# Gated layer of a two-layer decoder step: the v product with the tokens as the stationary operand

## The chip, the cores and the metric

One core of one Trainium2 chip. The metric is the device time of one execution in microseconds (us); lower is better. TensorE is called PE in the rows (PEld its weight loads), VectorE DVE, ScalarE ACT, GpSimd POOL and SyncE SP.

## The reference, cut to what matters

Layer 0 of the two layers is the gated one. Its input is 1024 prompt tokens and 64 sample tokens of width 1024; `a` is 2048 wide.

```python
h = rmsnorm(x, g)                          # x * r * g, r = 1/sqrt(mean(x*x) + eps) of each token
u, v, z = split(h @ w_in, 3, axis=-1)      # w_in 1024 x 6144, each part 2048 wide
v = rmsnorm(v, g_v)                        # over the 2048 channels of a token
mixed = einsum('gts,bnsgd->bntgd', tril(w_s), v in chunks of 128 tokens) + b_s
y = u * mixed * silu(z)
x = x + y @ w_out
```

The sample tokens' normed v rows are an output of their own. All products are of fp32 precision: each operand is split into a high part (the value rounded to fp32r) and a low part (the rest), and three products are added up, high x high, low x high, high x low.

## The kernel before, in words

**Groups and units.** The gated layer runs over two groups of tokens: group 0 has the 64 sample tokens and prompt chunks 0 to 3 (576 columns, taken by PE as two halves of 288), group 1 has chunks 4 to 7 (512 columns). Weights come in units of 512 KB, 1024 elements a partition. Each unit goes through a two-deep ring: SP loads `wraw` (L602), ACT rounds it to `whi` (`split_hi`, L429), POOL subtracts to get `wlo` (`split_lo`, L434), PE multiplies (`gemm`, L446). `split_hi` of unit u waits for PE to be through with unit u-2 (`w_used`), and the load of unit u waits for `wlo` of unit u-2. A group has 16 units of v, then 32 of z and u in turn (z, u, then the spatial mixing of one 128-channel strip f, at L2047 and L2051), then 16 of w_out.

**The v product.** The weights are the stationary operand, so v comes out channel-major, 128 channels x n tokens, for each strip f. ACT takes it out of PSUM (`v_out_of_psum`, L925), PE turns it with 4 transposes, and a fifth for the sample tokens (L1992, L1998), and DVE stores the token-major result in `v_raw` (L1344, L1347). After the last strip ACT squares `v_raw` tile by tile over all 2048 channels to get the sums (L938), takes the root (L941), and DVE inverts it to `rv` (L1362), scales the sample rows for their output with `gvb` (L1365) and the first strip for the mixing (L1380).

**The start.** SP loads nine tiles of x (L616; `xearly` for tiles 0 to 4, which are group 0, `xlate` for 5 to 8). PE turns tiles 0 to 4 (L1961) and DVE copies them into `xT` (L1308). ACT squares the tiles (L883) and takes roots (L888); DVE inverts them and spreads them on a diagonal (L1314 to L1320), PE spreads that over the partitions (L456). Then for each of the 8 channel blocks k: DVE makes `hfa` = x * g * r (L553), ACT its high part `hhi_g` (L539), DVE its low part `hlo_g` (L559), and PE's first v unit goes block by block behind them. The four late tiles are turned in the v loop, two transposes a strip (L1995), and copied by DVE (L1351).

**POOL's queue.** It holds, in this order: constants, the small loads (`gn`, the factor g, at L738, and others), `split_lo` of unit 0, a wait for the last x tile (`x_in[8]`), the loads of `wsraw`, `bsb` and `gvb` (L752 to L755), `split_lo` of units 1 to 16, then a wait for the turned mixing weights (`ws_ev`), their causal mask (L770), eight small DMAs that build `wsbd` (L774), and `split_lo` of unit 17 and on. Unit 16 is the first z unit, unit 17 the first u unit.

Of the kernel before, what the change touches and what calls it, by code (L numbers as in the profile page):

```python
# [17 lines left out]
F32 = mybir.dt.float32  # L18
F32R = mybir.dt.float32r
# [7 lines left out]
P = 128  # L27
# [26 lines left out]

GROUPS = [(0, 576, 4, True, 2), (576, 512, 4, False, 1)]
# [63 lines left out]
def hybrid_trunk(nc, x_prompt, x_sample, cache_k, cache_v, cache_ik, page_table, p_prompt, p_sample,  # L119
# [5 lines left out]
    with ctx:  # L125
# [61 lines left out]
        hfa = pl("hfa", [P, 2, GW])  # L187
        sqa = rbc
        yhi = nc.alloc_sbuf_tensor_at("yhi", [P, KA, 5 * P], F32R, offset=V0)
        vtmp = [szt, t1a]  # L190
        pl = region(Y0, Y0 + KA * GW * 4)
        xlate = pl("xlate", [P, 4, D])
        sqdump = pl("sqdump", [P, D], BF16)
        vdump = nc.alloc_sbuf_tensor_at("vdump", [P, KA, P], F32, offset=Y0)
        v_out = nc.alloc_sbuf_tensor_at("v_out", [NS, AW], F32, offset=Y0 + KA * P * 4)
        wsraw = pl("wsraw", [P, NGRP, P])
        gvb = pl("gvb", [NS, AW])
        xearly = nc.alloc_sbuf_tensor_at("xearly", [P, 5, D], F32, offset=V0)
# [116 lines left out]
        def as3(ap):  # L315
# [9 lines left out]
        x_tr, x_sq, x_ev, x_rt, x_dg = (sem(n) for n in ("x_tr", "x_sq", "x_ev", "x_rt", "x_dg"))  # L325
        gn_in = sem("gn_in")
# [12 lines left out]
        gmlp = {n: sem(f"A_{n}") for n in ("vev", "vtr", "vst", "vsq", "rv", "vs", "mix", "mt", "sz", "ut",  # L339
                                           "y", "yhi", "ylo", "xup")}  # L340
        sA = [Turn(gmlp, {n: g * {"vsq": 5, "rv": 1, "xup": KD}.get(n, KA) for n in gmlp}) for g in range(2)]
# [80 lines left out]


# [173 lines left out]
        def _(sp):  # L597
# [13 lines left out]

            for j in range(9):
                c0, n = tile_cols(j)
                src = (x_sample.rearrange("b t d -> (b t) d") if j == 0
                       else x_prompt[0, CHUNK * (j - 1):CHUNK * j, :])
                sp.dma_start(xtile(j)[0:n, :], src).then_inc(x_in[j], 16)  # L616
                if j == 4:
                    unit(0, 0, slab(w_in_a[0], 0, AW))
                    unit(1, 1, slab(w_in_a[0], 0, AW + P))
            for g in range(2):  # L620

                with sp.Fori(1 if g == 0 else 0, KA // 2) as i:
                    for ff in range(2):
                        unit(ff, U_A[g] + 2 * i + ff, pair(w_in_a[0], AW, i, ff))
# [100 lines left out]
        def _(pool):  # L725
# [6 lines left out]
            nc.gpsimd.memset(sv[:], 1.0).then_inc(cst, 1)  # L732
            own.link(nc.gpsimd.memset(ident[:], 0.0))
# [21 lines left out]
            pool.dma_start(gvb[:], g_v_a[0].partition_broadcast(NS)).then_inc(gvb_in, 16)  # L755
# [6 lines left out]
            for g in range(2):  # L762
                c0, n, _, _, np_ = GROUPS[g]
                for base, trips in ((U_A[g], KA // 2), (U_A[g] + KA, KA)):
# [3 lines left out]
                    if base == 0:  # L768
                        pool.wait_ge(ws_ev, 2)
# [96 lines left out]
        def _(act):  # L866
            own = Tally(act, av)
            for name, free in (("vev", 2), ("sz", 1)):
                act.sem_inc(gmlp[name], free)
# [4 lines left out]
            act.wait_ge(cst, 7)  # L874
# [16 lines left out]
            def norm_act(act, s, hi):  # L891
                for k in range(KD):
                    norm_hi(act, s, k, *hi)
                    if k == 5:
                        split_hi(act, 1, 1, 1)
                    if k in (4, 6):
                        x_square(3 + k // 2)
                for j in range(7, 9):
                    x_square(j)

            for j in range(5):
                x_square(j)
            x_roots(0, 5)
            split_hi(act, 0, 1, 0)
# [8 lines left out]
            for g in range(2):  # L913
                c0, n, nch, has_s, np_ = GROUPS[g]
                h = n // np_
                s = sA[g]
                if g == 0:
                    norm_act(act, nA[g], group_hi(g))
                else:
                    split_unit(U_A[g] + 1)  # L920

                def v_out_of_psum(f, ff):
                    act.wait_ge(w_used, U_A[g] + f + 1)
                    act.wait_ge(s["vtr"], s.at("vtr", f + 1))
# [1624 lines left out]
```

## Time and profile before

| what | value |
|---|---|
| median of 3 runs (lowest, highest) | 1977.17 us (1976.70, 1978.89) |
| span of the profiled execution, first to last instruction | 1973.8 us |
| mean granted TensorE clock, as a share of 2.4 GHz | 0.975 |
| PE busy | 1863.0 us, 94% of the span |
| DVE, ACT, POOL busy | 862.2, 793.2, 649.9 us |

The runs agree within 0.11%. Of the profiled execution only the span is recorded; the median lies 3.4 us above it, which is taken as what lies around the span. The gated layer fills about the first 850 us: group 0's v product from 18 to 139 us, group 1's from 484 to 581 us.

### The profile page before, as it was taken

Reading aid. Unit: us, or ns where it says so; the run is one execution under the profiler, and the core shown is the slowest. Engines: PE = TensorE matmul, PEld = TensorE weight load, DVE = VectorE, ACT = ScalarE, POOL = GpSimd, SP = SyncE. Lnnn points to the kernel's source line nnn. Section 1 sums busy time; section 2 is a strip of 40 time slices with the busy share of each in tenths; the row PEclk is TensorE's granted clock in tenths of the full one; section 3 lists DMA queues with packets and bytes.
Section 4 is the critical chain, followed back from the end, with each engine's and each line's share of the span. In section 5 each row is a group of like instructions: output and inputs, shape, how many; then the busy total and the mean of one; then the engine's idle time right before and its main releaser. Section 6 shows DMA issues by size and latency. Waiting matters only on the chain. (4 is left out here: it accounts for less than half of the span.)

```text
span 1973.8 us, 30722 instructions
## 1 busy us (share of the span) xinstructions
PE 1863.0 (94%) x11000; PEld 1647.2 (83%) x11000; DVE 862.2 (44%) x1653; ACT 793.2 (40%) x1148; POOL 649.9 (33%) x397
## 2 busy tenths in 40 slices
PE   7999999899999999999979989999989998699998
PEld 7999999899887888779969549999966765499997
DVE  4113333311114444033254877687778634512433
ACT  4233333212243333233235675567865554402211
POOL 4333323265333334654522131111132002354220
PEclk9999999999999999999989899999999999899999
DMA  6223222222222222331123110312231006531111
GB/s 187 75 65 85 74 74 74 64 77 83 85 85 85 85 85 86 95 109 33 32 64 122 31 56 22 89 43 66 88 121 31 1 1 209 186 99 43 44 55 45
DMA packets 226179, 150.76 MB, mean 76 GB/s; under 512 B 16754, under 2 KB 219250, under 8 KB 225714
## 3 DMA queue, kind: packets, MB, share of 16 engines
q1 hardware_dynamic: 210754, 125.78, 21.6%
q0 software_dynamic: 5152, 14.48, 2.4%
q10 hardware_dynamic: 10192, 9.46, 1.4%
q8 instruction: 46, 0.75, 0.2%
q14 instruction: 35, 0.29, 0.1%
HBM read 133.24 MB, written 16.43 MB: 76 GB/s over the span
## 5 line engine op out<-in xcount | busy, mean ns | idle before, releaser
L434 POOL TENSOR_TENSOR wlo<-wraw,whi 128x1024 fp32r<-128x1024 f32 x177 | 430.2, 2431 | 722.4 <-ACT whi L429 720.3
L446 PE MATMUL PS<-hhi_g,whi 128*128 128x288 f32 (+1 forms) x1152 | 324.0, 335 | 12.2 <-POOL wlo L434 7.2
L429 ACT ACTIVATE whi<-wraw 128x1024 fp32r<-128x1024 f32 x177 | 186.6, 1055 | 343.0 <-PE PS L446 324.6
L446 PE MATMUL PS<-hhi_g,wlo 128*128 128x288 f32 (+1 forms) x1152 | 317.1, 330 | 0.0
L446 PE MATMUL PS<-hlo_g,whi 128*128 128x288 f32 (+1 forms) x1152 | 316.9, 329 | 0.0
L446 PE MATMUL PS<-hhi,whi 128*128 128x364 f32 x1176 | 269.7, 338 | 12.8 <-DVE hlo L559 6.8
L446 PE MATMUL PS<-hlo,whi 128*128 128x364 f32 x1176 | 262.0, 331 | 0.0
L446 PE MATMUL PS<-hhi,wlo 128*128 128x364 f32 x1176 | 260.6, 330 | 0.0
L446 PEld LDWEIGHTS PS<-hhi_g,whi 128*128 128x128 f32 x1152 | 195.7, 189 | 31.1 <-issue 6.6
L446 PEld LDWEIGHTS PS<-hhi,whi 128*128 128x128 f32 x1176 | 204.0, 191 | 20.4 <-issue 13.9
L446 PEld LDWEIGHTS PS<-hhi_g,wlo 128*128 128x128 f32 x1152 | 196.4, 189 | 17.7
L446 PEld LDWEIGHTS PS<-hlo_g,whi 128*128 128x128 f32 x1152 | 196.9, 190 | 16.2
L446 PEld LDWEIGHTS PS<-hlo,whi 128*128 128x128 f32 x1176 | 206.5, 190 | 0.0
L446 PEld LDWEIGHTS PS<-hhi,wlo 128*128 128x128 f32 x1176 | 206.3, 190 | 0.0
L446 PE MATMUL PS<-yhi,whi 128*128 128x288 f32 (+1 forms) x384 | 108.0, 335 | 5.3 <-POOL wlo L434 4.7
L1387 DVE TENSOR_TENSOR t2a<-PS,szt 128x576 f32<-128x576 f32 (+1 forms) x32 | 23.2, 725 | 198.9 <-PE PS L446 198.3
L446 PE MATMUL PS<-yhi,wlo 128*128 128x288 f32 (+1 forms) x384 | 106.0, 330 | 0.0
L446 PE MATMUL PS<-ylo,whi 128*128 128x288 f32 (+1 forms) x384 | 105.3, 329 | 0.0
L1626 DVE TENSOR_SCALAR_CACHE_REDUCE acc<-sc,thr 128x384 bf16<-128x384 f32 (+1 forms) x124 | 100.7, 812 | 4.1
L1344 DVE COPY v_raw<-PS 128x512 f32 x32 | 22.1, 691 | 176.7 <-PE PS L1998 91.2
L988 ACT ACTIVATE sig<-hfb 128x1092 f32<-128x1092 f32 x16 | 17.9, 1118 | 174.7 <-DVE hfb L1441 174.5
L1423 DVE TENSOR_TENSOR xT<-PS,xT 128x576 f32<-128x576 f32 (+1 forms) x16 | 11.6, 725 | 168.0 <-PE PS L446 168.0
(392 smaller groups left out, 2726.4 us busy)
## 6 DMA issues: line engine op xcount, KB each, us to landing
wraw<-in_w_in_a_dram SPq DMA_DIRECT2D x96, 512.0 KB, 3.9
wraw<-in_w_out_a_dram SPq DMA_DIRECT2D x32, 512.0 KB, 4.0
wraw<-in_w_in_b_dram SPq DMA_DIRECT2D x25, 512.0 KB, 3.7
wraw<-in_w_pe_gate_dram SPq DMA_DIRECT2D x16, 512.0 KB, 4.2
kpg<-in_cache_k_dram SPq DMA_DIRECT2D x64, 128.0 KB, 2.8
vpg<-in_cache_v_dram POOLq DMA_DIRECT2D x64, 128.0 KB, 2.4
xs<-xT SPq DMA_DIRECT2D x1, 4368.0 KB, 12.6
xT<-xs SPq DMA_DIRECT2D x1, 4368.0 KB, 14.0
```

The source lines that it names most:

```text
L429: nc.scalar.activation(whi[par][:], wraw[par][:], ACT.Copy).then_inc(w_hi, 1)
L434: nc.gpsimd.tensor_tensor(wlo[par][:], wraw[par][:], whi[par][:].bitcast(F32), ALU.subtract).then_inc(w_lo, 1)
L446: mm = nc.tensor.matmul(o, w[par][:, k, :], r(k, c0, cn), start=first and i == 0 and n == 0, stop=last and i == KD - 1 and n == 2)
L988: nc.scalar.activation(sig[:], tg, ACT.Sigmoid).then_inc(s["sig"], 1)
L1344: vdst = nc.vector.tensor_copy(v_raw[:, bass.ds(f, 1), 0:4 * P].rearrange("p o n -> p (o n)"), PS[:, 4 + 2 * ff, :])
L1387: nc.vector.tensor_tensor(t2a[:, 0:n].rearrange("p (b n) -> p b n", b=np_), PS[:, 2:2 + np_, 0:h], szt[:, 0:n].rearrange("p (b n) -> p b n ...
L1423: nc.vector.tensor_tensor(x, PS[:, b:b + np_, 0:h], x, ALU.add).then_inc(s["xup"], 1)
L1626: own.link(nc.vector.tensor_scalar(vdmp[:, 0:(b + 1) * P], area(b), thr[:, b - 2:b - 1], None, ALU.is_lt, ALU.add, accum_out=cnt[:, b - 2: ...
```

## The change

In both groups the v product is made token-major at once: a tile of 128 tokens (all 1024 input channels, in 8 blocks k) is the stationary operand and 512 columns of the weights move past it. The 2048 channels are done in four rounds r of 512; a round has four units, each with the weights of two blocks k and 512 columns, still 1024 elements a partition. One PSUM bank holds 128 tokens x 512 channels over the four units of a round. In group 0 the 64 sample tokens form a tile of their own, whose stationary operand is the high and the low part side by side (64 + 64 columns) in `vpair`, with two products instead of three; the upper 64 partitions of the result are added to the lower by ACT (`vlow`) and DVE.

Group 0's v product uses xg = x * g without r. DVE multiplies by r (per token, so per partition) as it takes v out of PSUM. The early tiles are copied by ACT instead of DVE, multiplied by g, and split, tile by tile. The normed `hhi_g`, `hlo_g` of group 0, which z and u need, are made in the third round; the late x tiles, the spreading of r and the turning of the mixing weights are put between v units, at bank 7. The squares of v are summed round by round. Group 1's v loop is written out on PE, ACT, DVE and SP. The load of `gvb` moves behind the last v unit. The diff, cut to its core:

```diff
+NRND = 4
+EARLY_BANK = (5, 3, 1, 5, 3)
...
+        def v_tiles(g):
+            return ([(4, NS)] if g == 0 else []) + [(c, P) for c in range(4)]
+        def v_bank(g, r, t):
+            return (5 * r + t) % 7 if g == 0 else (4, 5, 0, 1, 2, 3, 6, 7)[4 * (r % 2) + t]
...
 SP
+            def v_load(g, m):
+                u, r, q = U_A[g] + m, m // NRND, m % NRND
+                if u >= 2:
+                    sp.wait_ge(w_lo, u - 1)
+                src = w_in_a[0][2 * P * q:2 * P * (q + 1), AW + BANK * r:AW + BANK * (r + 1)]
+                sp.dma_start(v_weight(wraw, m), src.rearrange("(k p) c -> p k c", p=P)).then_inc(w_raw[m % 2], 16)
+            V_AFTER = {2: 0, 4: 1, 6: 2}
                 sp.dma_start(xtile(j)[0:n, :], src).then_inc(x_in[j], 16)
-                if j == 4:
-                    unit(0, 0, slab(w_in_a[0], 0, AW))
-                    unit(1, 1, slab(w_in_a[0], 0, AW + P))
+                if j in V_AFTER:
+                    v_load(0, V_AFTER[j])
...
 POOL
-            pool.dma_start(gvb[:], g_v_a[0].partition_broadcast(NS)).then_inc(gvb_in, 16)
                     if base == 0:
+                        pool.wait_ge(w_used, KA)
+                        pool.dma_start(gvb[:], g_v_a[0].partition_broadcast(NS)).then_inc(gvb_in, 16)
                         pool.wait_ge(ws_ev, 2)
...
 ACT, group 0 before the rounds
+                    early_copy(0)
+                    early_copy(1)
+                    early_hi(0)
+                    early_copy(2)
+                    early_hi(1)
+                    early_copy(3)
+                    split_unit(0)
+                    early_hi(2)
+                    early_copy(4)
+                    early_hi(3)
+                    early_hi(4)
+                    split_unit(1)
+                    for j in range(5):
+                        x_square(j)
+                    x_roots(0, 5)
+                    split_unit(2)
...
 ACT, both groups
-                    nc.scalar.activation(vdump[0:rows], v_raw[0:rows, :, c * P:(c + 1) * P], ACT.Square,
-                                         accum_out=sv[0:rows, c:c + 1]).then_inc(s["vsq"], 1)
+                for r in range(NRND):
+                    if has_s:
+                        v_done(act, g, r, 0)
...
+                        nc.scalar.activation(vlow[:], PS[NS:P, v_bank(g, r, 0), :], ACT.Copy,
+                                             scale=rxs[NS:P, 0:1]).then_inc(s["vlw"], 1)
+                    for t in range(nt - 1):
+                        v_square(r, t)
+                    split_unit(U_A[g] + NRND * r + 5)
+                    v_square(r, nt - 1)
+                    for m in range(6, 9) if r < NRND - 1 else ():
+                        split_unit(U_A[g] + NRND * r + m)
+                        if g == 0 and r == 1 and m >= 7:
+                            r_copy(m - 7)
+                        if g == 0 and r == 2:
+                            for k in range(3 * (m - 6), min(3 * (m - 5), KD)):
+                                norm_hi(act, nA[0], k, *group_hi(0))
...
 DVE
+            dve.wait_ge(gn_in, 32)
+            early_scale(0)
+            for j in range(1, 5):
+                early_scale(j)
+                early_lo(j - 1)
+            early_lo(4)
...
+                for r in range(NRND):
+                    if g == 0:
+                        for piece in ((0, 1), (2, 3, 4, 5), (6, 7), ())[r]:
+                            late_copy(piece)
+                    v_round(r)
+                    if g == 0 and r == 2:
+                        ws_copy(0)
+                        dve.wait_ge(x_ev, 7)
+                        for k in range(KD + 1):
+                            norm_tile(dve, nA[0], k, c0, n, *group_tile(0))
+                        ws_copy(1)
+                dve.wait_ge(s["vsq"], s.at("vsq", NRND * len(tiles)))
+                nc.vector.reduce_sum(sv[:], vsum[:], axis=AX.X).then_inc(s["rv"], 1)
...
 PE
+                        for kk in range(2):
...
+                            if rows == NS:
+                                x = vpair[:, k].rearrange("p h n -> p (h n)")
+                                products = ((x, hi), (x, lo))
+                            else:
+                                a, b = ((vhi, vlo), (hhi_g, hlo_g))[g]
+                                a, b = a[:, k, c * P:(c + 1) * P], b[:, k, c * P:(c + 1) * P]
+                                products = ((a, hi), (b, hi), (a, lo))
...
+                BETWEEN = {1: (late_transpose, 0), 2: (late_transpose, 1), 3: (late_transpose, 2), 4: (late_transpose, 3),
+                           5: (late_transpose, 4), 6: (late_transpose, 5), 7: (late_transpose, 6), 8: (late_transpose, 7),
+                           9: (r_spread, 0), 10: (r_spread, 1), 11: (ws_transpose, 0), 12: (ws_transpose, 1)}
+                for m in range(KA):
+                    v_unit(m)
+                    if g == 0 and m in BETWEEN:
...
                 if g == 0:
+                    pe.wait_ge(s["vst"], 18)
+                    pe.wait_ge(nA[0]["lo"], KD)
```

`v_transpose`, `v_out_of_psum` and the strip loops of v go. `late_transpose` is 4 transposes, `ws_transpose` is 4, `r_spread` one product of 288 columns, as many in all as before. `early_scale` multiplies a tile of x by g, `early_hi` and `early_lo` split it. `v_round` takes the tiles of a round out of PSUM.

## Rows read from the trace of the kernel before

**Rows 1.** The profile's page, its first row: busy time, share, instructions.

```profile
PE 1863.0 (94%) x11000; PEld 1647.2 (83%) x11000; DVE 862.2 (44%) x1653; ACT 793.2 (40%) x1148; POOL 649.9 (33%) x397
```

**Rows 2.** Timeline of PE, one v unit of group 0: start, length, instruction, releaser.

```profile
43.88 0.60 PE L1992 MATMUL PS<-ident,t1a 128*128 128x128 f32 x4
...
44.91 0.42 PE L446 MATMUL PS<-hlo_g,whi 128*128 128x288 f32 x2
...
50.99 0.60 PE L1992 MATMUL PS<-ident,szt 128*128 128x128 f32 x4
```

**Rows 3.** Timeline of PE, one v unit of group 1.

```profile
501.31 0.60 PE L1992 MATMUL PS<-ident,t1a 128*128 128x128 f32 x4
...
501.98 0.40 PE L446 MATMUL PS<-hlo_g,whi 128*128 128x512 f32 x1
...
507.35 0.60 PE L1992 MATMUL PS<-ident,szt 128*128 128x128 f32 x4
```

**Rows 4.** Timeline of all engines, the start.

```profile
3.70 1.99 POOL L738 DMA_DIRECT2D gn<-in_g_norm_dram  x2 [0.31 <-POOL wsbd L736]
...
13.66 1.06 ACT L429 ACTIVATE whi<-wraw 128x1024 fp32r<-128x1024 f32 x1 [1.22 <-DMA wraw<-in_w_in_a_dram]
...
18.25 0.82 PE L446 MATMUL PS<-hhi_g,whi 128*128 128x288 f32 x2 [2.58 <-DVE hlo_g L559]
...
23.43 0.75 DVE L559 TENSOR_TENSOR hlo_g<-hfa,hhi_g 128x576 fp32r<-128x576 f32 x1
...
23.66 0.90 POOL L752 DMA_DIRECT2D wsraw<-in_w_s_a_dram  x1 [6.51 <-DMA xlate<-in_x_prompt_dram]
...
25.67 2.38 POOL L434 TENSOR_TENSOR wlo<-wraw,whi 128x1024 fp32r<-128x1024 f32 x1
...
26.46 2.88 DVE L559 TENSOR_TENSOR hlo_g<-hfa,hhi_g 128x576 fp32r<-128x576 f32 x2
...
28.73 0.53 PE L446 MATMUL PS<-hhi_g,whi 128*128 128x288 f32 x2 [1.92 <-DVE hlo_g L559]
...
37.45 0.51 PE L446 MATMUL PS<-hhi_g,whi 128*128 128x288 f32 x2
```

**Rows 5.** The tile `gn` (g), its two loads: time from issue to landing.

```profile
DMA to landing us min/median/max: 6.2/6.3/6.5
```

**Rows 6.** Windows at the start: stretch, length, engines' busy time, PEclk, DMA share, GB/s.

```profile
20.00:22.00 2.00, 2.00 (x10) 1.94 (x9) 1.96 (x4) 0.68 (x1) 0.00 (x0) 0.50 1.01 392
```

**Rows 7.** The profile's page, DMA issues: size, median us from issue to landing.

```profile
wraw<-in_w_in_a_dram SPq DMA_DIRECT2D x96, 512.0 KB, 3.9
```

**Rows 8.** Timeline of all engines, group 0 from v to z and u.

```profile
138.89 0.51 PE L446 MATMUL PS<-hhi_g,whi 128*128 128x288 f32 x2
...
141.05 1.09 POOL L770 TENSOR_SCALAR_AFFINE_SELECT wsT<-wsT 128x1024 f32<-128x1024 f32 x1 [7.52 <-DVE wsT L1358]
...
149.38 0.52 PE L446 MATMUL PS<-hhi_g,whi 128*128 128x288 f32 x2 [3.90 <-POOL wlo L434]
...
150.62 2.34 DVE L1365 SCALAR_TENSOR_TENSOR v_out<-v_raw,rv,gvb 64x2048 f32<-64x2048 f32 x1
...
157.36 1.05 PE L2047 MATMUL PS<-wsT,vs 128*128 x8
...
159.29 0.53 PE L446 MATMUL PS<-hhi_g,whi 128*128 128x288 f32 x2 [0.52 <-POOL wlo L434]
```

**Rows 9.** Timeline of all engines, group 1: v begins, then from v to z and u.

```profile
484.07 0.39 PE L446 MATMUL PS<-hhi_g,whi 128*128 128x512 f32 x1
...
581.10 0.48 PE L446 MATMUL PS<-hhi_g,whi 128*128 128x512 f32 x1
...
593.46 1.15 PE L2047 MATMUL PS<-wsT,vs 128*128 x8 [0.93 <-DVE vs L1380]
...
597.37 0.79 PE L446 MATMUL PS<-hhi_g,whi 128*128 128x512 f32 x1 [2.76 <-POOL wlo L434]
...
600.48 0.39 PE L446 MATMUL PS<-hlo_g,whi 128*128 128x512 f32 x1
```

More of the change, by code:

```diff
@@ L616, in _ @@
                 sp.dma_start(xtile(j)[0:n, :], src).then_inc(x_in[j], 16)
[L617 to L619 removed]
+                if j in V_AFTER:
+                    v_load(0, V_AFTER[j])
             for g in range(2):
[L622 to L624 removed]
+                for m in range(3 if g == 0 else 0, KA):
+                    v_load(g, m)
                 with sp.Fori(0, KA) as i:
@@ L889, in x_roots, with early_copy, early_hi @@
                                      scale=1.0 / D).then_inc(x_rt, 1)
[L891 to L904, printed above, removed]
+            def early_copy(j):
+                c0, n = tile_cols(j)
+                b = EARLY_BANK[j]
+                act.wait_ge(x_tr, j + 1)
+                nc.scalar.activation(xT[:, :, c0:c0 + n], PSF[:, b * BANK:(b + 2) * BANK]
+                                     .rearrange("p (k t) -> p k t", k=KD)[:, :, 0:n], ACT.Copy).then_inc(x_ev, 1)
+            def early_hi(j):
+                n = tile_cols(j)[1]
+                act.wait_ge(x_g, j + 1)
+                nc.scalar.activation(early_part(vpair, vhi, 0, j), xg[:, j % 2, :, 0:n], ACT.Copy).then_inc(x_hi, 1)
             def split_unit(u):
@@ L916, in _ @@
                 s = sA[g]
+                tiles = v_tiles(g)
+                nt = len(tiles)
                 if g == 0:
-                    norm_act(act, nA[g], group_hi(g))
+                    early_copy(0)
[14 more added lines that the diff above has]
+                    split_unit(2)
+                    for j in range(5, 7):
+                        x_square(j)
+                    split_unit(3)
+                    for j in range(7, 9):
+                        x_square(j)
+                    split_unit(4)
@@ new lines, in r_copy, with v_square @@
+                def r_copy(c):
+                    a, m = group_cols(0)[c]
+                    act.wait_ge(nA[0]["sum"], c + 1)
+                    nc.scalar.activation(rbc[:, a:a + m], PS[:, 7, 0:m], ACT.Copy).then_inc(x_ev, 1)
+                def v_square(r, t):
+                    c, rows = tiles[t]
+                    n = nt * r + t
+                    act.wait_ge(s["vst"], s.at("vst", n + 1))
+                    if n:
+                        act.wait_ge(s["vsq"], s.at("vsq", n))
+                    nc.scalar.activation(vdump[0:rows].rearrange("p (f d) -> p f d", d=P),
+                                         v_raw[0:rows, 4 * r:4 * r + 4, c * P:(c + 1) * P], ACT.Square,
+                                         accum_out=vsum[0:rows, c, r:r + 1]).then_inc(s["vsq"], 1)
@@ new lines, in late_transpose, with r_spread @@
+                def late_transpose(n):
+                    j, half = LATE[n]
+                    pe.wait_ge(x_in[j], 16)
+                    if n:
+                        pe.wait_ge(x_g, 5 + n)
+                    for k in range(4):
+                        tr = nc.tensor.transpose(PS[:, 7, k * P:(k + 1) * P],
+                                                 xlate[:, j - 5, (4 * half + k) * P:(4 * half + k + 1) * P], ident[:])
+                    tr.then_inc(x_tr, 1)
+                def r_spread(c):
+                    a, m = group_cols(0)[c]
+                    if c:
+                        pe.wait_ge(x_ev, 6)
+                    else:
+                        pe.wait_ge(x_dg, 2)
+                        pe.wait_ge(x_g, 5 + len(LATE))
+                    nc.tensor.matmul(PS[:, 7, 0:m], ones[:], acc[:, a:a + m], start=True, stop=True).then_inc(nA[0]["sum"], 1)
```

246 lines of the change are left out of this document (135 added, 111 removed).

## The prediction

> **What bounds the kernel now.** I read the page first: PE is busy for 94% of the span [rows 1], so the kernel is bound by what PE issues and by the short waits between. The other engines matter only where PE waits for them. Then I read the timelines, since busy time does not say what a matmul costs when they are pipelined: the cost is the distance from one start to the next. In group 0's v unit 23 pairs of 288-column matmuls fill 44.91 to 50.99 [rows 2], so a pair takes 0.264 us and one matmul 0.132 us. In group 1's, 23 matmuls of 512 columns fill 501.98 to 507.35 [rows 3]: 0.2335 us each. A unit with its transposes takes 50.99 - 43.88 = 7.11 us in group 0 and 507.35 - 501.31 = 6.04 us in group 1. Last, the two places where the v product hands over to z and u, and the start: there PE waits for others, and there the reader should look at what ACT and POOL have in front of the instruction that PE needs.
>
> **Columns and transposes, group 0.** Before: 16 units x 48 matmuls x 0.132 = 101.5 us. After: a unit has 4 tiles x 2 blocks x 3 products and 2 blocks x 2 products for the sample tile, 28 matmuls of 512 columns; 16 x 28 x 0.2335 = 104.6 us. The padded sample tile costs about 3 us. A unit is 28 x 0.2335 = 6.54 us. Removed: per unit, 7.11 - 48 x 0.132 = 0.77 us for 7 transposes, 0.11 us each; five of the seven go, 16 x 5 x 0.11 = 8.8 us; the other two and the 8 of the mixing weights are only moved.
>
> **Group 1.** 24 matmuls of 512 columns a unit, before and after, 5.60 us. The four transposes, 6.04 - 5.60 = 0.44 us a unit, go: 7.0 us.
>
> **Price of a matmul after.** The trace has no matmul with x stationary. Its nearest row is group 1's, same width, same types, a weight load before every matmul, one bank after another product in the same bank [rows 3]: 0.2335 us. From below, the columns' time at 2.4 GHz, 512 / 2.4 = 213 ns; from above, the pace that the rows show for 512 columns at the low clock does not apply, so I bound it by 5% more, 0.245 us. With 832 matmuls these ends are -17 and +10 us. I take the row.
>
> **The start.** Before, PE's first v unit starts at 18.25 [rows 4] and crawls behind the normalisation: two units and one set of transposes are done at 37.45. After, nothing of the norm is ahead, but DVE's first instruction waits for `gn`. Its second load is issued about 4.8 us (half way in the row at 3.70) and lands 6.3 us later [rows 4, 5], so at 11.1. ACT waits with it, since `early_hi(0)` stands ahead of `early_copy(2)`. From there: scale 0.7, high part 0.6 (64 columns x 8), copy 2, high part 1, copy 3 and the rounding of unit 0 at 1.06 each [rows 4], POOL 2.4 [rows 4], some 0.5 for hops and for a DVE instruction in POOL's way: 11.1 + 0.7 + 0.6 + 4.2 + 2.4 + 0.5, rounded up to 19.7. So PE starts 1.4 us later than before. PE is idle for some us before that and starts at the lower clock of 1.2 GHz, as it does now (0.50 at 20 to 22 us, [rows 6]; the first pair at 18.25 takes 0.82 us, one at 37.45 0.51, [rows 4]). I let it have that clock for the first 5 us, about as now: 11 matmuls of 0.43 us (512 / 1.2), the other 17 take 4.0: unit 0 ends at 28.6. The low parts of tiles 2 to 4, on DVE at 1.3 us an instruction (0.75 x 1024 / 576 [rows 4]), are done by 24 and are not waited for.
>
> Unit 1 needs `wlo` from POOL, and there stands the wait for the last x tile. SP now queues the load of unit 2 ahead of x tiles 7 and 8, and it waits for `split_lo` of unit 0, at 19.7. Three loads of 512 KB on an idle queue: 3.9 us for the first to land [rows 7], then 1.3 us each at 392 GB/s [rows 6]: 26.3. Then two issues (0.90 and about 0.6) and `split_lo` 2.4: 30.2. PE waits 28.6 to 30.2. Unit 1 ends at 36.7, and with `late_transpose(0)` 0.44 the third unit starts at 37.2, against 37.45. The start gains nothing: the time that the norm took goes to g's load, and then to the late x tile.
>
> **Rest of group 0's v.** 14 units x 6.54 = 91.6, ten sets of four transposes less the one counted, 9 x 0.44 = 4.0, two `r_spread` at 0.45: 37.2 + 91.6 + 4.9 = 133.7 for the end of v, against 138.89 [rows 8]. ACT has some 1 us of squares a tile beside its split in a unit of 6.5 us, and is not late. In the last units DVE makes the normed tiles: two instructions of 0.8 for each k, three k a unit. They end, with the last evacuations that PE waits for (`vst` 18), about 1.5 us behind the last v matmul, which is hidden as follows.
>
> **Handover in group 0.** What u needs is `split_lo` of unit 17, behind POOL's mask and eight DMAs. Before, POOL's mask starts at 141.05 and PE's u at 149.38, 8.3 us later [rows 8]. After, POOL may only begin when the last v unit is through, and has the `gvb` load (0.6) first: 133.7 + 0.65 + 8.3 = 142.7. z takes 6.35 and fits in front. PE's wait is then 1 to 2.6 us where it was 3.9, so I take the clock to hold; before, the u unit took 157.36 - 149.38 = 7.98 instead of 6.35, 1.6 us for the lower clock.
> DVE's two-input instructions and POOL's subtraction block each other: two `hlo_g` took 2.88 us with a POOL instruction in progress, where one takes 0.75 [rows 4]. DVE's `v_out`, 2.34 us [rows 8], now waits for the moved `gvb` load, some 5 us after its issue, and so comes about when POOL wants `split_lo` 17. Price 0 to 2.3 us; I take 1.0. The Trainium skill, "SBUF — State Buffer", section "SBUF: two separate sides", says that a DVE instruction with two SBUF inputs and a GpSimd one that reads SBUF take a shared port as an exclusive lock, whoever starts first; the two rows agree, and by it the loss here is all of what is left of `v_out` or nothing.
> So u starts at 143.7, mixing at 150.1, and 1.4 us later (157.36 to 159.29 less the 0.52 wait) z of strip 1, at 151.5, against 159.29. **Group 0 gains 7.8 us.**
>
> **Handover in group 1.** Before, ACT squares four tiles over 2048 channels after v, with the splits of units 2 and 3 of z and u behind them. POOL waits for them, PE waits 0.93 for `vs` and 2.76 for `wlo` [rows 9], and then runs 7 matmuls in 3.11 us (597.37 to 600.48) where full clock needs 1.63: 1.5 us more. After, three quarters of the squares are done in the earlier rounds; after v there are one split, one square (under 1 us), a root with two table loads, 5.4 us in all, inside z's 5.60. All these waits go. From the first v matmul to z of strip 1 it was 597.37 + 1.5 - 484.07 = 114.8; it becomes 16 x 5.60 + 2 x 5.60 + 0.8 = 101.6. **Group 1 gains 13.2 us**, of which 7.0 are transposes and 5.2 the waits and the clock; 1.0 is the last, uncovered transposes and the slow first matmul behind each set.
>
> **Sum.** 7.8 + 13.2 = 21.0 us. The profiled span of 1973.8 becomes 1952.8; the median 1977.17 becomes 1956.2. Everything later only moves forward.
>
> **The rivals.** A change within 0.2% (4 us) cannot be told from none here.
> *The start and the handover cost more* (0.17): `gn` lands later beside the earlier weight loads, the clock falls again in the 1.6 us gap before unit 1 and in the one before u (1.6 us each), `v_out` blocks POOL fully. Together 5 to 9 us: 1961 to 1965. For it: ACT's and DVE's order is strict and long. Against: a gap of 1.92 us before 28.73 left the pair there at 0.53 us, the full clock's length [rows 4], while one of 3.9 did not [rows 8].
> *Matmuls are faster* (0.08): with 512 columns from the contiguous weight tile they come near 213 ns; up to 17 us more, 1940 to 1950. Against it, both widths show the same loss over 2.4 GHz (0.132 for 288 / 2.4 = 0.120 us, 0.2335 for 0.213).
> *Slower than before* (0.05): a matmul with x stationary costs more, because each load of the array is now a new tile. It decides at 21.0 / 832 = 25 ns, a matmul of 0.26 us; at 0.27 the time is 1986. Against it: group 1 reloads the array for each matmul already and the load is hidden.
> *No change* (0.03): PE's time is not what sets the end, and the gain is given back. Against it: PE at 94%, and later stages have no deadline of their own.
> *As forecast* (0.67): 1951 to 1961.
>
> **How the numbers follow.** Forecast 1956.2. The range takes in the start's and handover's bounds above, and below half of the faster matmul: 1949 to 1965. Faster by over 0.2%: 0.67 + 0.17 + 0.08 = 0.92; within: 0.03; slower: 0.05.
>
> **What would show it.** First v matmul near 19.7, waiting for POOL; a PE gap before unit 1 ended by POOL; a v period of 6.54 in group 0 and 5.60 in group 1 with no transposes; z near 133.7 to 135.2; u released by POOL near 143; in group 1 no PE wait between v and strip 1. A v matmul distance off 0.2335, or ACT or POOL late in each round, would make it wrong.

## The result, and the profile after

The changed kernel takes 1949.51 us (median of 4 runs, 1948.35 to 1950.51), the kernel before 1978.03 in the same comparison: ratio 0.9857, 95% interval 0.9844 to 0.9869, so it is 28.5 us faster (25.9 to 30.9). The forecast was 1956.2 us and a gain of 21.0; the time lies at the lower end of the range, 1949 to 1965. The changed kernel run again as an experiment gave 1948.51. Around a span lie 1.6 us (the run of 1948.35 us has a span of 1946.7), not the 3.4 that I had taken from the kernel before, whose traced execution was itself 1.8 us shorter than the median; so spans are compared with spans below, and medians with medians.

The page of the changed kernel, its first row (busy time, share, instructions; before: [rows 1]). PE has 464 matmuls and 23 us less, and is still busy for 94%:

```profile
PE 1839.6 (94%) x10536; PEld 1608.9 (83%) x10536; DVE 877.7 (45%) x1641; ACT 795.0 (41%) x1186; POOL 652.8 (34%) x398
```

Its timeline, all engines, of the start (before: [rows 4]). Columns: start, length, instruction, in brackets the idle time before it and who ended it:

```profile
11.76 1.83 DVE L1400 TENSOR_TENSOR xg<-xT,gn 128x512 f32<-128x512 f32 x2 [11.76 <-DMA gn<-in_g_norm_dram]
...
16.91 3.27 POOL L474 TENSOR_TENSOR wlo<-wraw,whi 128x1024 fp32r<-128x1024 f32 x1 [6.09 <-ACT whi L469]
...
17.90 3.37 DVE L1408 TENSOR_TENSOR vlo<-xg,vhi 128x1024 fp32r<-128x1024 f32 x1
...
20.24 0.79 PE L2143 MATMUL PS<-whi,vpair 128*128 128x512 f32 x1 [3.71 <-POOL wlo L474]
...
26.88 0.90 POOL L800 DMA_DIRECT2D wsraw<-in_w_s_a_dram  x1 [6.70 <-DMA xlate<-in_x_prompt_dram]
...
30.79 0.50 PE L2143 MATMUL PS<-whi,vpair 128*128 128x512 f32 x1 [1.37 <-POOL wlo L474]
31.13 0.39 PE L2143 MATMUL PS<-wlo,vpair 128*128 128x512 f32 x1
...
37.31 0.60 PE L2156 MATMUL PS<-ident,xlate 128*128 128x128 f32 x4
37.67 0.48 PE L2143 MATMUL PS<-whi,vpair 128*128 128x512 f32 x1
```

The reader is to see four predicted things. DVE's first instruction is released by `gn` (11.76; 11.1 was forecast). PE's first v matmul waits for POOL (20.24; 19.7). Unit 1 waits for POOL, which sat 6.70 us behind the last x tile (30.79; 30.2). The third unit begins at 37.67 (37.2). And one that was not: from 31.13 to 37.31 there are 27 matmuls, 0.2289 us each, where I had taken 0.2335 (group 1's row before).

The handover in group 0 (before: [rows 8]):

```profile
132.80 2.71 DVE L1459 TENSOR_SCALAR v_raw<-PS,rx 128x512 f32<-128x512 f32 x4
...
134.55 0.60 PE L486 MATMUL PS<-hhi_g,whi 128*128 128x288 f32 x2 [1.83 <-DVE v_raw L1459]
134.98 4.56 POOL L823 DMA_DIRECT2D wsbd<-wsT  x8 [0.29 <-POOL wsT L819]
...
138.51 2.34 DVE L1496 SCALAR_TENSOR_TENSOR v_out<-v_raw,rv,gvb 64x2048 f32<-64x2048 f32 x1
139.56 3.54 POOL L474 TENSOR_TENSOR wlo<-wraw,whi 128x1024 fp32r<-128x1024 f32 x1
140.78 3.18 DVE L1511 TENSOR_SCALAR vs<-v_raw,rv 128x128 f32 x5
143.15 0.53 PE L486 MATMUL PS<-hhi_g,whi 128*128 128x288 f32 x2 [0.45 <-POOL wlo L474]
...
150.94 0.53 PE L486 MATMUL PS<-hhi_g,whi 128*128 128x288 f32 x2
```

z waits 1.83 us for the last evacuations, u is released by POOL at 143.15 (143.7 was forecast), and z of strip 1 starts at 150.94 (151.5; before 159.29). `v_out` did cross `split_lo` of unit 17: 3.54 us where 2.4 is usual, a price of 1.1 us where I had put 1.0. Windows of the same stretch (columns: stretch, length, busy time of PE, PEld, DVE, ACT and POOL, PEclk, DMA share, GB/s) show what I had not granted, a fall of the clock behind the 1.83 us wait:

```profile
134.00:138.00 4.00, 3.45 (x15) 3.46 (x16) 1.68 (x4) 3.57 (x10) 3.71 (x7) 0.61 0.57 133
138.00:142.00 4.00, 4.00 (x31) 4.00 (x30) 3.69 (x3) 0.37 (x2) 3.98 (x4) 0.97 0.05 3
```

Group 1 (before: [rows 9]), its first v matmul, ACT behind v, and PE at mixing and strip 1:

```profile
475.75 0.39 PE L2143 MATMUL PS<-whi,hhi_g 128*128 128x512 f32 x1
...
563.90 1.06 ACT L469 ACTIVATE whi<-wraw 128x1024 fp32r<-128x1024 f32 x1
564.86 0.61 ACT L1006 ACTIVATE vdump<-v_raw 128x512 bf16<-128x512 f32 x1
...
566.88 0.30 ACT L1031 ACTIVATE rv<-sv,eps 128x5 f32<-128x5 f32 x1
...
574.84 1.06 PE L2214 MATMUL PS<-wsT,vs 128*128 x8
575.65 0.48 PE L486 MATMUL PS<-hhi_g,whi 128*128 128x512 f32 x1
```

One square is left behind v, and neither mixing nor strip 1 has a wait in brackets. From 475.75 to 575.65 are 99.9 us (forecast 101.6, before 114.8).

### The profile page after: what moved, and what is told of

The parts are those of the page before. It is cut to its first block and busy times, and to the rows that moved or that the text cites. A ratio compares the mean times of both kernels' runs of the same rounds, so it can differ in the third digit from the quotient of the medians.

```text
span 1946.7 us, 29415 instructions
## 1 busy us (share of the span) xinstructions
PE 1839.6 (94%) x10536; PEld 1608.9 (83%) x10536; DVE 877.7 (45%) x1641; ACT 795.0 (41%) x1186; POOL 652.8 (34%) x398
## 5 line engine op out<-in xcount | busy, mean ns | idle before, releaser
L486 PE MATMUL PS<-hhi_g,whi 128*128 128x288 f32 (+1 forms) x768 | 214.1, 333 | 2.3 <-DVE v_raw L1459 1.8
L486 PE MATMUL PS<-hhi_g,wlo 128*128 128x288 f32 (+1 forms) x768 | 210.7, 329 | 0.0
L486 PE MATMUL PS<-hlo_g,whi 128*128 128x288 f32 (+1 forms) x768 | 210.4, 328 | 0.0
L486 PEld LDWEIGHTS PS<-hhi_g,whi 128*128 128x128 f32 x768 | 129.9, 188 | 15.0 <-issue 2.3
L486 PEld LDWEIGHTS PS<-hhi_g,wlo 128*128 128x128 f32 x768 | 130.2, 188 | 11.8
L486 PEld LDWEIGHTS PS<-hlo_g,whi 128*128 128x128 f32 x768 | 130.6, 189 | 11.0
L1518 DVE TENSOR_TENSOR t2a<-PS,szt 128x576 f32<-128x576 f32 (+1 forms) x32 | 23.2, 725 | 206.7 <-PE PS L486 206.7
L486 PEld LDWEIGHTS PS<-yhi,whi 128*128 128x128 f32 x384 | 65.6, 190 | 16.5 <-POOL wlo L474 10.0
```

The lines of the kernel that those rows point to most:

```text
L486: mm = nc.tensor.matmul(o, w[par][:, k, :], r(k, c0, cn), start=first and i == 0 and n == 0, stop=last and i == KD - 1 and n == 2)
L1518: nc.vector.tensor_tensor(t2a[:, 0:n].rearrange("p (b n) -> p b n", b=np_), PS[:, 2:2 + np_, 0:h], szt[:, 0:n].rearrange("p (b n) -> p b n ...
```

## The experiments

Times are medians; "later" is the time from the z product of strip 1 in group 1 to the end of the span. All kernels here have the same instructions in it. Where that z product starts at the low clock behind a wait (the kernel before, experiments 1 and 2), its 1.5 us of slow matmuls are counted ahead of it.

**1. Group 1's v product as before, group 0's as changed.** Units of 512 columns with weights stationary and four transposes (code of before), squares behind v.

```diff
-                    v_load(g, m)
+                    if g == 0:
+                        v_load(g, m)
+                    else:
+                        unit(m % 2, U_A[g] + m, slab(w_in_a[0], 0, AW + m * P))
...
+                if g:
+                    for f in range(KA):
+                        old_unit(f)
+                        if f:
+                            old_transpose(f - 1)
+                    old_transpose(KA - 1)
```

> Group 0 as in the changed kernel, group 1's v product as before: weights stationary, 4 transposes a strip, squares after the last strip. Theory (the steps of the two traces): group 1 from its first v matmul to z of strip 1 goes from 99.9 us back to about 113.3 us plus up to 1.5 us of low clock, so the time lies 13.4 to 15 us above the changed kernel, and some 12 to 15 below the kernel before. Rival (the gain of the change beyond my sum sits in group 0 or is only the clock's luck in later stages): the time lies under 11 us above the changed kernel.

Measured: 1964.83 us (1964.10 to 1965.38), 15.3 over the changed kernel. The first v matmul of group 1 starts at 476.11 (475.75 in the changed kernel), and its timeline at strip 1 is:

```profile
585.52 1.15 PE L2268 MATMUL PS<-wsT,vs 128*128 x8 [1.00 <-DVE vs L1538]
589.44 0.79 PE L489 MATMUL PS<-hhi_g,whi 128*128 128x512 f32 x1 [2.77 <-POOL wlo L477]
```

With 1.5 for the low clock, strip 1's z is at 590.9, 15.3 behind 575.65. Group 1 itself takes 590.9 - 476.1 = 114.8 us, to 0.1 us what it took in the kernel before, against 99.9: 14.9 us, at the upper end of what the theory has; the other 0.4 lie ahead of group 1, where nothing is edited.

**2. Only group 1's squares behind v again**, four of 2048 channels; v itself as changed.

```diff
                 def v_square(r, t):
+                    if g:
+                        return
...
+                if g:
+                    act.wait_ge(s["vst"], s.at("vst", 4 * NRND))
+                    for c in range(nch):
+                        if c:
+                            act.wait_ge(s["vsq"], s.at("vsq", NRND * c))
+                        nc.scalar.activation(vdump_g1[:], v_raw[:, :, c * P:(c + 1) * P], ACT.Square,
+                                             accum_out=sv[:, c:c + 1]).then_inc(s["vsq"], NRND)
```

> Changed kernel, but in group 1 ACT squares v after the last round, four tiles of 2048 channels, as before, with the splits of the third and fourth z and u unit behind them. Theory: the waits of the old handover come back and only they: 0.9 us for vs, 2.8 for wlo and 1.5 of low clock, 5.2 us more than the changed kernel. Rival: the handover was paid by the transposes at the end and not by the squares: under 1.5 us more.

Measured: 1956.18 us (1955.25 to 1959.26), 6.7 over. Group 1 itself, from its first v matmul at 477.32 to 581.74 + 1.5, takes 105.9 us, 6.0 more than 99.9. PE's waits between 300 and 700 us (columns: engine, line, waited for: us in total, times, longest) and its timeline there:

```profile
PE PS L488 <- POOL wlo L476: 2.8, 1, 2.8
PE PS L2228 <- DVE vs L1525: 1.2, 1, 1.2
```

```profile
577.82 1.15 PE L2228 MATMUL PS<-wsT,vs 128*128 x8 [1.24 <-DVE vs L1525]
581.74 0.79 PE L488 MATMUL PS<-hhi_g,whi 128*128 128x512 f32 x1 [2.77 <-POOL wlo L476]
582.32 0.63 PE L488 MATMUL PS<-hlo_g,whi 128*128 128x512 f32 x1
```

Both waits of before and its slow matmuls are back. They belong to the place of the squares, not to the form of the v product.

**3. Order of the three products.** In the changed kernel one stationary tile is followed by another; here the x tile `a` is stationary twice in a row.

```diff
-                                products = ((a, hi), (b, hi), (a, lo))
+                                products = ((a, hi), (a, lo), (b, hi))
```

> Changed kernel with the three products of a tile and block ordered high x high, high x low, low x high, so that the same stationary tile is loaded twice in a row, as the weights were before. The v matmuls of the changed kernel follow each other at 0.229 us, those with the weights stationary at 0.2335. Theory A (the pace hangs on loading the same stationary tile again): the pace goes to 0.2335 and the time up by 3.7 us. Theory B (it hangs on which operand moves): pace 0.229, time within 1 us of the changed kernel.

Measured: 1949.74 us (1948.46 to 1950.43), the v matmuls at the same 0.229 us. Changing which load is repeated changes nothing: theory A is out. Theory B's number came, but its reason does not hold alone either. In experiment 5, below, the second v unit has the same form and the full clock, and its matmuls follow each other at 0.2335 us (20 starts in 4.67 us):

```profile
32.42 0.40 PE L2144 MATMUL PS<-whi,vhi 128*128 128x512 f32 x1
...
37.09 0.40 PE L2144 MATMUL PS<-wlo,vhi 128*128 128x512 f32 x1
```

Single units of experiments 2, 4, 7 and 10 do so too (in experiment 7 the one from 94.88), and experiment 10 is the kernel of experiment 6, which has none. All other v units of the changed form are at 0.229, and no product with x moving is. What sets the pace is open.

**4. x tiles 7 and 8 ahead of weight unit 2 on SP.**

```diff
-            V_AFTER = {2: 0, 4: 1, 6: 2}
+            V_AFTER = {2: 0, 4: 1, 8: 2}
```

> Changed kernel with SP's load of weight unit 2 moved behind x tiles 7 and 8, which then wait for nothing. Theory: POOL's wait for the last x tile ends some us earlier, PE's wait of 1.4 us before v unit 1 goes, and the time falls by 1.0 to 1.6 us. Rival: the x tiles come no earlier because the queue moves bytes all the time, or the earlier x tiles push back the first ones: no change.

Measured: 1947.63 us (1944.37 to 1950.56), 1.9 less, which the medians alone do not settle. In the trace PE's wait ahead of unit 1 is gone; PE's wait for `wlo` from 0 to 300 us (in the changed kernel 5.1 us in two waits):

```profile
PE PS L2143 <- POOL wlo L474: 4.6, 1, 4.6
```

Strip 1's z of group 1 comes at 573.00 against 575.65 and, repeated, 576.83. The queue that I named is the cause of the wait. Not all of the 2.65 us is the edit's: the first two v units, without PE's wait between them, take 14.4 us here and 15.7 in the changed kernel, but 14.6 in experiment 3 (only the order of the products) and 16.6 in experiment 9 (no edit). That is the length of the low clock, which differs from run to run.

**5. The gated layer's g ahead of everything on POOL.**

```diff
+            pool.dma_start(gn[:, 0, :], g_norm[0].rearrange("(f p) -> p f", p=P),
+                           allow_slow_non_contiguous=True).then_inc(gn_in, 16)
             nc.gpsimd.memset(ones[:], 1.0).then_inc(cst, 1)
```

> Changed kernel with the load of the factor g of layer 0 as POOL's first instruction and DVE's early tiles waiting for that load alone. In the changed kernel DVE's first multiplication starts at 11.8 us, when g lands, and PE's first v matmul at 20.2. Theory: g lands near 8 us, the chain of copies and splits is then held by x tile 3, which lands near 12, and the first v matmul comes 1 to 2 us earlier; but POOL's wait for the last x tile still holds v unit 1, whose load order hangs on the first split, so that tile lands earlier by as much: 1 to 2 us off the time. Rival: the chain is held by the x tiles anyway, within 0.5 us.

Measured: 1948.32 us (1945.60 to 1951.22), 1.2 less, not distinct from the changed kernel. PE's timeline shows where 1.4 us went:

```profile
18.83 0.79 PE L2144 MATMUL PS<-whi,vpair 128*128 128x512 f32 x1 [3.12 <-POOL wlo L474]
29.29 0.80 PE L2144 MATMUL PS<-whi,vpair 128*128 128x512 f32 x1 [2.25 <-POOL wlo L474]
```

v begins 1.4 us earlier (18.83 against 20.24), PE waits longer ahead of unit 1 (2.25 against 1.37), and has the low clock behind that wait. At strip 1's z of group 1 (575.64) all of it is spent.

**6. The handover in group 0.** z may start before the last evacuations (other banks), `gvb` is loaded by SP, mask and eight DMAs go ahead of `split_lo` 16, and `ws_copy(1)` goes earlier on DVE. With the banks, PE's waits for turned x tiles in the first unit move too.

```diff
-            return (5 * r + t) % 7 if g == 0
+            return (5 * r + t + 1) % 7 if g == 0
...
-                    pe.wait_ge(s["vst"], 18)
                     pe.wait_ge(nA[0]["lo"], KD)
...
-                        ws_copy(1)
+                            if k == 2:
+                                ws_copy(1)
```

> Changed kernel, group 0's handover from v to z and u: the banks of the rounds are one up so that z waits only for the normed tiles, the mixing weights are copied, masked and spread before POOL's split of unit 16, and SP loads g_v. In the changed kernel z waits 1.8 us for DVE and then has 3.4 us of low clock, and u waits 0.5 for POOL. Theory: z starts right behind v, u about 6.6 us later, no low clock: z of strip 1 comes 3 to 4 us earlier, the time falls by 3 to 4 us. Rival: POOL's eight DMAs between its splits hold unit 16 or DVE's sample output holds the first mixing, and the gain is under 1 us.

Measured: 1950.30 us (1949.02 to 1951.70), 0.8 over: a miss. Its timeline:

```profile
134.80 0.53 PE L486 MATMUL PS<-hhi_g,whi 128*128 128x288 f32 x2 [1.04 <-DVE hlo_g L599]
...
148.22 1.05 PE L2217 MATMUL PS<-wsT,vs 128*128 x8
...
150.18 0.53 PE L486 MATMUL PS<-hhi_g,whi 128*128 128x288 f32 x2 [0.54 <-POOL wlo L474]
```

```profile
134.00:138.00 4.00, 3.20 (x24) 3.21 (x25) 3.73 (x6) 2.60 (x7) 0.00 (x0) 1.00 0.75 155
```

The handover did get shorter: from z to mixing 13.42 us against 15.04, at a PEclk of 1.00, and the wait ahead of z 1.04 instead of 1.83. That is 2.4 us, less a new wait of 0.54 for POOL before strip 1: 1.9, not 3 to 4, since `hlo_g` is now what z waits for. But v ended at 133.76 instead of 132.72, 1.0 later, which is there already at its first matmul (21.26 against 20.24; in the repeat, experiment 10, it is at 20.55), and 4.5 went in stages without an edit: later is 1949.9 - 574.29 = 1375.6 us against 1946.7 - 575.65 = 1371.05.

**7. Experiments 4, 5 and 6 together.**

> The changed kernel with the x tiles ahead of weight unit 2, g loaded first and the new handover, all three. Theory: the gains add up, as they lie at places that follow each other on PE: 5.5 to 8 us off the changed kernel, near 1943. Rival: the start's two edits share one wait and give 1.5 together, 4 to 5 us in all.

Measured: 1943.98 us (1941.92 to 1946.24), ratio to the kernel before 0.9829 (0.9815 to 0.9843); 5.5 less than the changed kernel, and the fastest version here. Its timeline of PE:

```profile
18.29 0.50 PE L2147 MATMUL PS<-whi,vpair 128*128 128x512 f32 x1 [2.88 <-POOL wlo L474]
...
129.37 0.52 PE L486 MATMUL PS<-hhi_g,whi 128*128 128x288 f32 x2 [1.05 <-DVE hlo_g L599]
...
142.79 1.05 PE L2218 MATMUL PS<-wsT,vs 128*128 x8
...
144.75 0.53 PE L486 MATMUL PS<-hhi_g,whi 128*128 128x288 f32 x2 [0.55 <-POOL wlo L474]
```

No wait ahead of unit 1 is left, the handover again takes 13.42 us, and strip 1 is 6.2 us earlier than 150.94. The end of v is 4.4 us earlier (128.3 against 132.72), where experiment 4 alone had 2.8 at strip 1 and experiment 5 nothing: g's early load pays only once POOL does not stand behind an x tile. Of the 4.4, 1.9 are the earlier start of v, 1.4 the wait, and the rest is a shorter low clock. Strip 1's z of group 1 is at 569.41, so later is 1370.9 us, though this kernel has experiment 6's edit in it.

**8. The kernel before, once more.**

> The kernel before, once more, for its stages. From group 1's z of strip 1 to the end its first trace took 3.9 us longer than the trace of the changed kernel, though nothing there was changed; four variants of the changed kernel took 1.4 to 2 us less to 1.3 more than it. Theory A (where the low-clock stretches fall differs from run to run): this trace's later stages lie off the first one's by up to 3 us, and the waits and low-clock stretches fall at other places. Theory B (the kernel before is slower there for a reason of its own): again 3 to 5 us more than the changed kernel.

Measured: 1978.30 us, span 1976.7, 2.9 over the first trace's. 2.7 of it arise before z of strip 1 of group 0, where the clock stayed low in the start for longer:

```profile
29.94 0.85 PE L446 MATMUL PS<-hhi_g,whi 128*128 128x288 f32 x2 [1.78 <-DVE hlo_g L559]
...
162.02 0.53 PE L446 MATMUL PS<-hhi_g,whi 128*128 128x288 f32 x2 [0.51 <-POOL wlo L434]
...
600.23 0.79 PE L446 MATMUL PS<-hhi_g,whi 128*128 128x512 f32 x1 [2.76 <-POOL wlo L434]
```

Later is 1976.7 - 601.7 = 1375.0 us, and in the first trace 1973.8 - 598.9 = 1374.9: the same to 0.1 us. That is theory B's number, again some 4 us more than in the changed kernel; why is not shown by it.

**9. The changed kernel, once more.**

> The changed kernel once more, without an edit. Disputed: the gain measured is 28.5 us, but the first matmul of strip 1 of group 1's z product, behind which no instruction is changed, comes only 23.2 us earlier than in the kernel before; 3.9 us more appear in the unchanged stages behind it, where the granted clock of the kernel before fell oftener. Both traces of the kernel before spend 1386.3 us there. Theory A (the places where the clock falls are set by the program and its timing, and so are part of the effect): this run spends within 0.5 us of the first one's time (1376.9 us) there. Theory B (they fall anew in each run): it lies anywhere between 1375 and 1386 us, and the 3.9 us are the luck of two traces.

Measured: 1948.51 us (1947.14 to 1953.31), span 1946.6; strip 1's z of group 1 at 576.83, so later is 1369.8 us against 1371.05. (The 1376.9 and 1386.3 us of the expectation were counted from a matmul some 6 and 11 us earlier, so that in the kernel before they hold its waits at the handover too.) The two are 1.3 us apart, more than theory A's 0.5 and inside theory B's range, but both are 3.9 to 5.2 us shorter than both of before.

The traces show where the time goes. Counted from the end, the 3000th matmul lies 565.7 and 565.9 us before the end in the two traces of before, and 561.8 and 561.9 in those of the changed kernel: 4 us arise behind it. They arise mainly at a few places, where the granted clock differs. At the largest but one both kernels wait the same 2.07 us for the same tile; in the 5 us behind it the kernel before has the low clock for a part, the changed kernel has not. First before, then changed (windows as above):

```profile
1500.42 1.12 PE L2387 MATMUL PS<-rdiag,ones 128*128 128x512 f32 x2 [2.07 <-POOL rdiag L843]
1500.42:1505.42 5.00, 5.00 (x16) 3.41 (x17) 2.49 (x10) 2.87 (x7) 2.08 (x4) 0.66 0.38 105
```

```profile
1477.72 1.12 PE L2554 MATMUL PS<-rdiag,ones 128*128 128x512 f32 x2 [2.07 <-POOL rdiag L892]
1477.72:1482.72 5.00, 5.00 (x23) 3.57 (x24) 3.17 (x10) 3.83 (x8) 2.08 (x4) 1.00 0.32 108
```

16 matmuls against 23 in the same 5 us: 1.4 us. The largest, 1.6 us, is at 1652 us in before (a PEclk of 0.78 over 25 matmuls, 1.00 in the changed kernel), again behind waits of the same length, 2.03 and 1.88 us, in both.

**10. The handover kernel, once more.**

> The handover kernel once more. Its first trace reached strip 1 of the z product of group 0 earlier than the changed kernel, and its unchanged stages took 1381.4 us against 1376.9, which ate the gain. Theory A (set by the program): again about 1381.4 us. Theory B (anew in each run): it moves by some us, and with it the miss of the first run would be luck of its clock and no cost of the edit.

Measured: 1950.62 us, span 1949.0, strip 1's z of group 1 at 573.50: later is 1375.5 us, as in its first run (1375.6). Theory A's number. But experiment 7, with the same edit, has 1370.9, so it is not the edit of the handover that costs these 4 us.

**11. A delay of 22.5 us ahead of everything.**

```diff
+            for _ in range(18):
+                own.link(nc.gpsimd.memset(acc[:], 0.0))
             nc.gpsimd.memset(ones[:], 1.0).then_inc(cst, 1)
```

> The changed kernel with 18 more fills of a 128x1092 tile on POOL ahead of everything (about 1.0 us each and 0.25 us between them, 22.5 us in all), with nothing else changed: all work of the start waits for them except loads. If nothing but the arrival time matters to the later stages, they take what they take in the kernel before (1386.3 us) and the kernel is about as slow as the one before (1975 to 1978 us). If the later stages do not depend on when they begin, they take 1376.9 us as in the changed kernel; the time is then 1949.5 plus at most 22.5, 1968 to 1972 us (less where loads that are late today are now hidden, by 3 us or so).

Measured: 1963.91 us (1962.61 to 1966.04), span 1961.0. Timeline of PE:

```profile
22.21 7.21 PE L2092 MATMUL PS<-ident,xearly 64*128 64x64 f32 x40 [22.21 <-POOL ident L784]
35.53 0.80 PE L2145 MATMUL PS<-whi,vpair 128*128 128x512 f32 x1 [6.11 <-POOL wlo L474]
...
591.39 0.48 PE L486 MATMUL PS<-hhi_g,whi 128*128 128x512 f32 x1
```

The first v matmul is 15.3 us later, not 22.5: PE's waits for x, 7.7 us in the changed kernel, are hidden. Later is 1961.0 - 591.39 = 1369.6 us, as in experiment 9, though it begins 15 us later. So a start 15 us later does not bring back the 4 us; the time, 4 us under the range given, misses by the hidden loads alone.

**12. One such fill, 1.3 us.** The same edit with `range(1)`.

> The same with one such fill, 1.3 us. If the later stages take 1376.9 us whatever the shift, the span is 1947.5 to 1948.5 us. If a shift of about 1 us is enough to move the places where the clock falls, as the handover kernel's 1381.4 us would let one think, the later stages move by 1 us or more either way, and the span lies outside of that.

Measured: span 1947.6 us, strip 1's z at 576.75, later 1370.9 us (one run). A small shift did not move it either.

## Why the prediction was right, and where it was short

The forecast of direction and range held, the range by 0.5 us, and that with some luck: it went down to 1949 only as a margin for faster matmuls, while what filled it is a matmul 5 ns faster (3.9 us, as against up to 17 in that rival) and a change of some 4 us in later stages, for which the forecast had nothing. The measured time lies outside of the 1951 to 1961 called "as forecast" and in the bracket of the rival of faster matmuls. The sum was 7.5 us short against the medians: 6.1 between the first two traces (0.6, 1.7 and 3.9 in the rows below, rounded), the rest between these traces and the medians. The table has both traces of each kernel; gains are first against first, second against second.

| stretch | before, twice | changed, twice | gain | forecast |
|---|---|---|---|---|
| to z of strip 1, group 0 | 159.3, 162.0 | 150.9, 151.9 | 8.4, 10.1 | 7.8 |
| to z of strip 1, group 1 (before with 1.5 for its slow matmuls) | 439.6, 439.7 | 424.7, 424.9 | 14.9, 14.8 | 13.2 |
| later | 1374.9, 1375.0 | 1371.05, 1369.8 | 3.9, 5.2 | 0 |
| span | 1973.8, 1976.7 | 1946.7, 1946.6 | 27.1, 30.1 | 21.0 |

**The price of a matmul, the term with 832 in it.** I took 0.2335 us from group 1's row, within bounds of 0.213 and 0.245. It is 0.229 in nearly all units: 832 x 0.0047 = 3.9 us, 2.1 in group 0 and 1.8 in group 1. The rival of faster matmuls was right in sign and far too large in size. For group 1 this is the whole of 101.6 against 99.9. Experiment 3 excludes the order of the loads as its cause, and the unit of experiment 5 at 0.2335 shows that the form of the product does not fix it alone.

**The start.** Right step by step and within 0.8 us. (Two of its sums are loose: its terms give 19.5 us for the first v matmul, not 19.7, and 28.4 for the end of unit 0, not 28.6; neither reached the result, since POOL releases unit 1.) "The start gains nothing" held: 37.67 against 37.45. Experiments 4, 5 and 7 show that the two causes named, g's load and the x tile behind weight unit 2, are the true ones and worth 3.3 us together (1.9 and 1.4), 4.4 with the shorter low clock. What the forecast left out is that the start differs by a microsecond or two from run to run (first v matmul at 20.24 and 19.73; before, 18.25 and 19.61), with the clock behind its waits.

**The handover in group 0.** The chain over POOL held to 0.6 us (u at 143.15). The step "so I take the clock to hold" failed: the 1.83 us wait for the evacuations, which I had put at 1.5 and called hidden, brought one stretch at the low clock, and the z product took about 1.6 us longer. It cost little, because PE waits for POOL's `split_lo` 17 there in any case: PE's wait for it shrank to 0.45 from the 1 to 2.6 expected. Experiment 6 took the fall away (PEclk 0.61 to 1.00) and the handover became 1.6 us shorter from z to mixing. No experiment puts group 0's v product back as it was, so its gain of 8.4 to 10.1 us is read from the timelines of the two kernels and not taken apart by a run.

**Group 1.** Right. The gain of 14.9 is 7.0 of transposes, 5.2 of waits and clock, 1.0 of the rest and 1.8 of the matmul's price. Experiment 1 gives back these 14.9 us in group 1 with the old form; experiment 2 gives back 6.0 there with the squares alone, 0.8 more than the 5.2 booked for them.

**"Everything later only moves forward" failed.** It is the largest missing term, 3.9 to 5.2 us. Behind strip 1 nothing is edited, and before lags 23.2 us there, but 27.1 at the end. PE's longest waits in the last 570 us are the same in both kernels within 0.2 us each, and the difference arises where the granted clock falls behind such a wait in one kernel and not in the other (experiment 9's rows). The figures are 1374.9 and 1375.0 us in both runs of before, 1375.6 and 1375.5 in both of experiment 6, and in the other forms of the changed kernel 1371.05, 1369.8 (the repeat), 1372.9, 1370.6, 1372.5, 1369.8, 1371.1, 1370.9, 1369.6 and 1370.9 (experiments 1 to 5, 7, 11, 12). Experiment 3 changes only an order that costs nothing, and has 1372.5; experiment 7 has experiment 6's edit, and not its 1375.6. A later start is not the cause (experiments 11 and 12).

What decides it is open, and so is whether it belongs to the kernel at all. A repeat came back within 0.1 to 1.3 us, but with two traces each: the runs of one and the same kernel have spans of 1945.5 to 1951.7 us (changed) and 1973.1 to 1979.2 us (before), and what part of these 6 us lies in the later stages no trace shows. What stands is that the medians differ by 28.5 us, while the traces have 23.2 to 24.9 by strip 1 of group 1: some 4 us of the gain are measured on the average of many runs, and are not tied to anything that the change does.

**The rivals.** More cost in start and handover: a fall of the clock came, but ahead of z and at neither of the two places named, and was covered by POOL. Slower matmuls with x stationary, which would have decided at 25 ns: the sign is the other one, -4.7 ns. No change: PE stayed the bound at 94%, and experiment 1 shows group 1's part of the gain at the end of the run.

The low part of an early tile at 17.90, beside POOL's `wlo` from 16.91 to 20.18, takes 3.37 us, where 1.22 is its length alone. `v_out`, which started first at 138.51, kept its 2.34 us, and `split_lo` 17, which started at 139.56 when 1.3 us of it were left, took 3.54 where 2.4 is usual, 1.1 more. The rule cited with the handover (the Trainium skill, "SBUF — State Buffer", section "SBUF: two separate sides": a shared port pair held as an exclusive lock between a DVE instruction with two SBUF inputs and a GpSimd one that reads SBUF, by whichever starts first) agrees with both.

## What to carry to other kernels

Where one engine is busy for 94%, an edit is priced by the distance between its instructions' starts; with hundreds of them even 5 ns is a term, and a form that the trace doesn't show deserves a bound on both sides rather than the nearest row alone. Work that one engine does in one block behind a product (here the squares) belongs in the product's rounds: it was worth 6.0 us in group 1 (experiment 2), nearly the 7.0 of all the transposes that went. And an edit of 2 us can't be read from the total when unedited stages answer with 4 us of clock: compare the traces at a point just behind the edit, and trace both kernels several times before the rest is given a cause; two traces each were too few here.

## What was not expected of the hardware

- A 512-column matmul with the weight tile moving and x stationary mostly has a period of 0.229 us, with x moving 0.2335, in the same kernel and at the full clock; but single units of the first form run at 0.2335 as well (experiment 5 from 32.42 to 37.09).
- The length of a wait does not by itself tell whether the clock falls behind it: behind 1.37 us (the changed kernel at 30.79) and 2.40 us (experiment 11 at its second unit, 46.02) the matmuls kept the full clock, behind 1.83 us (134.55) and 2.25 us (experiment 5 at 29.29) they did not, and behind one and the same wait of 2.07 us they did in the changed kernel and not in the one before.
- `vs`, five instructions with one data input and a scalar for each partition, took 3.18 us beside POOL's `split_lo` (140.78 in the changed kernel, above) and 1.05 in experiment 6 with POOL idle; so not only DVE's instructions with two data inputs are slowed by it. Experiment 6:

```profile
143.78 1.05 DVE L1517 TENSOR_SCALAR vs<-v_raw,rv 128x128 f32 x5
```

- Unedited stages of 1370 us came back within 0.1 us in two kernels and within 1.3 us in a third, and differ by up to 6 us between kernels, at places where only the granted clock differs.
